# A mixture-of-experts encoder on one core: the last item's rows stay on chip, a zeroed row table, and ones-products ahead of the first transposes

## What is computed

```python
for i in range(DEPTH):                       # DEPTH = 2
    h = rmsnorm(x, norm_mix_g[i])
    x = x + (sgu_mixer(...) if i % 2 == 0 else pool_mixer(...))
    h = rmsnorm(x, norm_ffn_g[i])
    x = x + hierarchical_moe(h, ...)         # hid = silu(xb @ w_gate[e]) * (xb @ w_up[e]); hid @ w_down[e]
return rmsnorm(x, final_norm_g)
# end of hierarchical_moe: every token sums its two experts' rows, each times its gate weight
out = jax.ops.segment_sum(y_sorted * w_sorted[:, None], tok, num_segments=n_tok)
```

## Time and profile before

| | |
|---|---|
| time, median of 3 runs | 2081.47 us (2078.33 to 2082.1) |
| profiled execution: its time, its span | 2081.68 us, 2080.0 us |
| PE busy | 2022.5 us, 97% |
| DVE, ACT, POOL busy | 1576.7, 1363.6, 301.8 us |
| DMA | 559.38 MB, mean 269 GB/s |
| mean granted clock of TensorE | 0.984 |

### The profile page before, as it was taken

The page is one execution under the profiler, slowest core; times in us unless marked ns, Lnnn a source line. Parts: engine busy times, 40 slices in busy tenths (PEclk is TensorE's granted clock), DMA queues, the critical chain, the costliest instruction groups (busy, mean ns, idle before and its releaser), DMA issues.

```text
span 2080.0 us, 31898 instructions
## 1 busy us (share of the span) xinstructions
PE 2022.5 (97%) x9663; PEld 1680.3 (81%) x9663; DVE 1576.7 (76%) x1933; ACT 1363.6 (66%) x1744; POOL 301.8 (15%) x343
## 2 busy tenths in 40 slices
PE   8999999999999999999999989998899999999996
PEld 6888888888788888888888868887688888888883
DVE  4334553426579999999999986867899999999995
ACT  4442244434438888888888874325688888888884
POOL 1000000000002322222222200000133222222110
PEclk9999999999989999999999989998899999999999
DMA  7322223323449999999999983243799999999996
GB/s 278 100 93 81 82 91 101 94 91 116 148 164 348 385 384 377 387 388 371 379 382 384 393 311 137 90 151 132 287 347 378 380 381 382 375 379 385 397 366 260
DMA packets 163754, 559.38 MB, mean 269 GB/s; under 512 B 28472, under 2 KB 29728, under 8 KB 161648
## 3 DMA queue, kind: packets, MB, share of 16 engines
q1 hardware_dynamic: 138960, 510.72, 64.8%
q0 software_dynamic: 22416, 39.30, 5.3%
q10 hardware_dynamic: 2320, 8.62, 1.1%
HBM read 541.21 MB, written 51.97 MB: 285 GB/s over the span
## 4 chain that ended last, share of the span: by engine, by line
PE 90%; DVE 5%; DMA 2%; ACT 1%; issue 1%; SPq 0%; ACTq 0%; DVEq 0%; POOLq 0%
PE bank L628 28%; PE bank L630 27%; PE bank L629 27%; PE bank L893 3%; PE bank L708 2%; PE bank L931 1%; DMA sbias<-y_rows 1%; PE bank L751 1%; PE bank L642 1%; DVE big L1490 1%; DVE w_lo L1482 1%; ACT w_hi L1069 0%; DMA raw<-in_a_w_out 0%; DVE vbias L1540 0%; PE bank L697 0%
## 5 line engine op out<-in xcount | busy, mean ns | idle before, releaser
L628 PE MATMUL bank<-w_hi,a_hi 128*128 128x512 f32 x2072 | 822.3, 397 | 6.1 <-DVE a_lo L1482 2.5
L630 PE MATMUL bank<-w_hi,a_lo 128*128 128x512 f32 x2072 | 809.8, 391 | 0.0
L629 PE MATMUL bank<-w_lo,a_hi 128*128 128x512 f32 x2072 | 807.2, 390 | 0.0
L1482 DVE TENSOR_TENSOR w_lo<-raw,w_hi 128x1024 fp32r<-128x1024 f32 x372 | 454.4, 1225 | 333.8 <-ACT w_hi L1069 308.8
L1069 ACT ACTIVATE w_hi<-raw 128x1024 fp32r<-128x1024 f32 x372 | 392.9, 1060 | 436.7 <-PE bank L630 421.9
L1482 DVE TENSOR_TENSOR w_lo<-big,w_hi 128x1024 fp32r<-128x1024 f32 x530 | 620.0, 1219 | 26.3 <-ACT w_hi L1069 20.8
L1069 ACT ACTIVATE w_hi<-big 128x1024 fp32r<-128x1024 f32 x530 | 549.4, 1063 | 107.6 <-PE bank L630 91.7
L628 PEld LDWEIGHTS bank<-w_hi,a_hi 128*128 128x128 f32 x2072 | 390.4, 188 | 85.2 <-issue 3.3
L630 PEld LDWEIGHTS bank<-w_hi,a_lo 128*128 128x128 f32 x2072 | 389.3, 188 | 83.8
L629 PEld LDWEIGHTS bank<-w_lo,a_hi 128*128 128x128 f32 x2072 | 390.2, 188 | 77.4
L1482 DVE TENSOR_TENSOR a_lo<-bank,a_hi 128x512 fp32r<-128x512 f32 x211 | 137.7, 683 | 32.5 <-ACT a_hi L1069 32.5
(11 more groups left out here) (222 smaller groups left out, 1589.1 us busy)
## 6 DMA issues: line engine op xcount, KB each, us to landing
big<-in_w_gate SPq DMA_DIRECT2D x260, 512.0 KB, 5.7
big<-in_w_up SPq DMA_DIRECT2D x254, 512.0 KB, 5.6
raw<-in_w_down SPq DMA_DIRECT2D x244, 512.0 KB
raw<-in_a_w_in SPq DMA_DIRECT2D x64, 512.0 KB, 3.9
raw<-in_a_w_out SPq DMA_DIRECT2D x32, 512.0 KB, 3.3
big<-y_rows SPq DMA_DIRECT2D x12, 1024.0 KB, 7.3
big<-in_w_down SPq DMA_DIRECT2D x16, 512.0 KB
raw<-in_b_w_in SPq DMA_DIRECT2D x16, 512.0 KB, 4.4
```

What stands on the lines that cost most here:

```text
L628: pe.matmul(dst, left_hi, right_hi, start=first, stop=False)
L629: pe.matmul(dst, left_hi, right_lo, start=False, stop=False)
L630: return pe.matmul(dst, left_lo, right_hi, start=False, stop=last)
L1482: return nc.vector.tensor_tensor(dst, src, f32(hi), ALU.subtract)
```

## The change

1. Layer 1's last item is no longer scattered. Its rows stay in SBUF as `last_hi` (ACT) and `last_lo` (DVE). DVE compares an index row, which PE makes as ones times `tri` in bank 7, with each row's token number and writes eight 0/1 matrices of 128x128, `last_oh`. PE multiplies them with the rows for each of the eight tiles (`add_last`).
2. In layer 1 SP's pair loads wait for the last but one item's scatter. As the last item's rows are then missing from `y_rows`, ACT fills the whole of `y_rows[1]` with zeros early in the kernel.
3. `PE_TILES` are now 1, 3, 4, 6, 7 and `DVE_TILES` 0, 2, 5. Tiles 6 and 7 reuse banks of tiles 1 and 3.
4. PE makes 60 products of ones at the start. For that `tri` holds ones at first; its true values are cast later, ahead of the second round's evictions. The identity is loaded alone, and the rest of `cf` goes on SP's queue behind x.
5. The pooling mixer uses the semaphores of the SGU's ring.

```diff
-PE_TILES, PE_PAIR = (1, 3, 5, 6), (0, 6, 2, 4)
-DVE_TILES = (0, 2, 4, 7)
+PE_TILES, PE_PAIR = (1, 3, 4, 6, 7), (0, 6, 2, 0, 6)
+DVE_TILES, DVE_PAIR = (0, 2, 5), 4
+WARM = 60
...
+            sp.dma_start(cf[:, P:C_ALL], A["c_float"][:, P:C_ALL]).then_inc(g.consts, 16)
...
-                sp.wait_ge(M.scattered, 16 * n)
+                sp.wait_ge(M.scattered, 16 * n if L == 0 else 16 * (n - 1))
+                if L == 1:
+                    sp.wait_ge(M.lo, ROUND * n)
...
+            pool.memset(zeros, 0.0).then_inc(g.init, 1)
...
-                scatter_rows(n - 1, meta_g, end_y)
+                if L == 0:
+                    scatter_rows(n - 1, meta_g, end_y)
...
-            pe.wait_ge(g.consts, 16)
-            pe.wait_ge(g.gain_first, 16)
+            pe.wait_ge(g.eps, 2)
+            for _ in range(WARM):
+                pe.matmul(bank[6][:, 0:P], tri[:, :], tri[:, :], start=True, stop=True)
+            pe.wait_ge(g.gain_first, 32)
...
+                if L == 1:
+                    pe.matmul(bank[7][:, 0:P], ones[:, :], tri[:, :], start=True, stop=True).then_inc(g.iota, 1)
                 down(n - 1, lambda j: pe.wait_ge(M.lo, ROUND * n + j + 1), end_h_hi, end_h_lo, 4)
...
+            def add_last(b, t, first):
+                for c in range(2):
+                    for part in (last_hi, last_lo):
+                        done = pe.matmul(bank[b + c][:, :], last_oh[:, t * P:(t + 1) * P], part[:, c, :],
+                                         start=first and part is last_hi, stop=part is last_lo)
+                return done
...
+            for i in range(3):
+                begin_sum(i)
+            pe.wait_ge(g.moved, TT + 2)
+            for t in range(TT):
+                if t in DVE_TILES:
+                    d = DVE_TILES.index(t)
+                    if d:
+                        pe.wait_ge(g.d_added, 2 * d)
+                    add_last(DVE_PAIR, t, True).then_inc(g.pe_summed, 1)
+                else:
+                    i = PE_TILES.index(t)
+                    if i > 2:
+                        begin_sum(i)
+                    landed, count = pair_landed(1, t)
+                    upper, lower = pair_rows(1, t)
+                    pe.wait_ge(landed, count)
+                    add_rows(PE_PAIR[i], False, False, upper)
+                    add_rows(PE_PAIR[i], False, False, lower)
+                    add_last(PE_PAIR[i], t, False).then_inc(g.pe_summed, 1)
...
-            act.dma_start(cf[:, :], A["c_float"]).then_inc(g.consts, 16)
+            act.dma_start(ident, A["c_float"][:, C_ID:C_ID + P]).then_inc(g.gain_first, 16)
...
+                if hf == 0:
+                    act.wait_ge(g.init, 3)
+                    act.dma_start(y_rows[1].rearrange("(a p) d -> p a d", p=P),
+                                  zeros.rearrange("p (o d) -> p o d", o=1).to_broadcast([P, 2 * TT, D])).then_inc(g.zeroed, 16)
...
-                weighted_rows(end_y, 4, meta_g)
+                weighted_rows(end_y if L == 0 else last_hi, 4, meta_g)
...
+                        if hf == 0:
+                            dve.wait_ge(g.consts, 16)
+                            nc.vector.tensor_copy(tri[:, :], cf[:, C_TRI:C_TRI + P]).then_inc(g.cast, 1)
+                            dve.wait_ge(g.cast, 1)
...
+                    for t in range(TT):
+                        nc.vector.tensor_scalar(last_oh[:, t * P:(t + 1) * P], bank[7][:, 0:P], tile_token[:, t:t + 1], None, ALU.is_equal) \
+                            .then_inc(g.moved, 1)
+                    for c in range(2):
+                        dve.wait_ge(M.y_out, 2 * (n - 1) + c + 1)
+                        nc.vector.scalar_tensor_tensor(last_lo[:, c, :], bank[4 + c][:, :], meta_g[:, 2:3].bitcast(F32), f32(last_hi[:, c, :]),
+                                                       ALU.mult, ALU.subtract).then_inc(g.moved, 1)
```

More of the change, by code:

```diff
@@ L157, in encoder_trunk @@
         end_y = xg.rearrange("p (n f) -> p n f", n=2)
+        last_hi, last_lo = a_hi[:, 3:5, :], a_lo[:, 3:5, :]
+        last_oh = a_hi[:, 5:7, :].rearrange("p a t -> p (a t)")
+        last_token, tile_token = cols[:, 16:17], cols[:, 24:24 + TT]
+        zeros = bu[:, 1024:2048]
         moe_raw = [bu[:, n * UNIT:(n + 1) * UNIT] for n in range(GU)] + [raw[:, n, :] for n in range(DN)]
@@ L243, in encoder_trunk @@
                        "eps", "sq", "std", "rstd", "waited", "hn", "t_full", "t_hi", "t_lo", "out_stored", "last_dn",
-                       "pe_summed", "pe_added",
+                       "pe_summed", "pe_added", "zeroed", "iota", "moved", "d_added",
                        "fold_raw", "fold_left", "fold_hi", "fold_lo", "fold_full", "fold_out", "fold_stored"],
@@ L250, in encoder_trunk @@
                  {"raw": RING})
-        q = sems("pool", RINGS + ["full", "ev_act", "ev_dve", "chain", "d_ready", "d_hi", "d_lo"],
-                 {"raw": RING})
+        q = sems("pool", RINGS + ["full", "ev_act", "ev_dve", "chain", "d_ready", "d_hi", "d_lo"], {})
         ROUTE = ["rw_ready", "x_t", "lg_full", "lg_read", "slots", "slot_oh", "ids_full", "first", "w_full", "tab", "weighted",
@@ L1045, in add_rows, with begin_sum @@
                 return done
-            for b, t in zip(PE_PAIR, PE_TILES):
-                if b == 2:
-                    pe.wait_ge(m[1].y_out, 2 * (n - 1))
[L1050 to L1058, removed]
+            def add_last(b, t, first):
[4 more added lines that the diff above has]
+                return done
+            def begin_sum(i):
+                if i == 1:
+                    pe.wait_ge(g.moved, TT)
+                if i == 2:
+                    pe.wait_ge(m[1].y_out, 2 * (n - 1))
+                if i > 2:
+                    pe.wait_ge(g.pe_added, 2 * (i - 2))
+                add_rows(PE_PAIR[i], True, False, x_res[:, PE_TILES[i], :])
+            for i in range(3):
[9 more added lines that the diff above has]
+                    i = PE_TILES.index(t)
+                    if i > 2:
+                        begin_sum(i)
[5 more added lines that the diff above has]
+                    add_last(PE_PAIR[i], t, False).then_inc(g.pe_summed, 1)
         Q_V = HALVES * BF
@@ L1071, in split @@
             def split(M, slot_raw, slot, src, loads, used):
-                act.wait_ge(M.raw[slot_raw], 16 * loads)
+                act.wait_ge(s.raw[slot_raw], 16 * loads)
                 act.wait_ge(M.used, used)
@@ L1174, in _ @@
                 root(0, t)
-            act.wait_ge(g.gain_first, 18)
+            act.wait_ge(g.gain_first, 34)
             for hf in range(HALVES):
@@ L1714, in _ @@
             nc.vector.memset(eps, EPS).then_inc(g.eps, 1)
[L1715 to L1718, removed]
+            nc.vector.memset(tri[:, :], 1.0).then_inc(g.eps, 1)
+            dve.wait_ge(g.gain_first, 33)
             nc.vector.tensor_copy(mix_gain, bank[7][:, 0:KC]).then_inc(g.gain_first, 1)
-            dve.wait_ge(g.gain_first, 18)
+            dve.wait_ge(g.gain_first, 34)
             dve.sem_inc(s.ev_dve, BANKS)
@@ L2101, in _, with add_last, norm_last @@
             dve.wait_ge(g.gain_ready, 16 * 4)
[L2102 to L2107, removed]
+            def add_last(t):
+                d = DVE_TILES.index(t)
+                dve.wait_ge(g.pe_summed, t + 1)
+                for c in range(2):
+                    x = x_res[:, t, c * 512:(c + 1) * 512]
+                    nc.vector.tensor_tensor(x, bank[DVE_PAIR + c][:, :], x, ALU.add).then_inc(g.d_added, 1)
+                dve.wait_ge(g.d_added, 2 * d + 2)
+            def norm_last(t):
+                normed_tile(8 + t // HT, t // HT, t // HT * HT, t % HT, t // HT)
+            add_last(0)
+            add(1, 0)
+            add_last(2)
+            norm_last(0)
+            add(1, 2)
+            norm_last(1)
+            norm_last(2)
+            add_last(5)
+            norm_last(3)
+            norm_last(4)
+            add(1, 5)
+            for t in (5, 6, 7):
+                norm_last(t)
 _SHAPES = ((1, SEQ, D), "float32")
```

17 lines of the change are left out of this document (12 added, 5 removed).

## The result

The changed kernel takes 2083.22 us (median of 22 runs, 2078.64 to 2085.76), the kernel before 2080.55 us (22 runs on the same chips, 2078.33 to 2082.51). The ratio is 1.0012 with a 95% interval of 1.0006 to 1.0017: 2.7 us slower, under the 0.2% that the forecast called no change. The forecast was 2091 us. The profiled execution has a span of 2081.9 us, 2080.0 before. TensorE (PE) was busy for 98% of it.

What follows compares the result with a forecast made beforehand. PE, busy for 97% of the span, was taken as the bound. 2080.0 - 1.8 (start) + 6.9 (stall) + 1.5 (half clock) + 3.0 (end) = 2089.6 of span, so 2091 us; the range takes in 2081.5 and 2095.

Steps and rivals of the forecast that it cites:

- So I let it go first: Near 20 us: the 8.39 MB zeros store takes all DMA engines for 20.5 us ahead of SP's loads; unit 10 lands at 61.
- +6.9 us of stall: Second round of the main loop: PE wants the bank at 58.3, free only at 65.2; range 6.6 to 9.2.
- +1.5 of half clock: Behind PE's stall: half the clock for 3.0 us, as after the old end's 5.8 us of idling, loses 1.5 us.
- The row that I trusted: Old profile, 547 to 550.5 us: all 290 data packets were a 2 MB store's; a 512 KB load came after it.
- The row at 630.5 to 633.5: Old profile, equal 512 KB pieces: the queues shared, ACT's having 44.0% of the engines' time; cited for even sharing.
- Start, -1.8: Kernel start: ones-products quicken the transposes, moving PE's first main-loop product from 16.56 to about 14.8; 0 to -2.3 us.
- End, +3.0: Last item: loads start 5.4 us sooner, but PE's 27.5 us of sums make scaling end at 2079.3; range 2 to 4.5.
- the queues share evenly: Rival, near 20 us: SP's loads are through by 54, just in time for 58.3, no stall; 2082.9 us, chance 0.30.
- the forecast's main path: Near 20 to 65 us: zeros first, with the PE stall, giving a slower kernel at 2091 us; chance 0.64.
- Decides at an identity sum under 0.64: Faster rival, kernel end: PE's chain under 22 us keeps the tail's 5.4 us; 2074.5 us, chance 0.06 with others under 2077.

Runs made afterwards that it cites:

- e7: The changed kernel itself, profiled once more without an edit: 2081.42 us, one run.
- e1: The kernel before with only the start part of the change, no zeros store and the old end: 2078.48 us, ratio 0.9989.
- e4: The changed kernel with the last sums split 4 and 4 tiles between PE and DVE: 2084.31 us, ratio 1.0021.
- e2: The changed kernel with the zeros store issued behind the first v tiles (about 66 us), not behind the third unit: 2081.32 us, ratio 1.0007.
- e9: The kernel before with only the memset, the zeros store behind ACT's third unit and its wait: 2082.27 us, ratio 1.0004.
- e8: The changed kernel with late zeros, last sums split 4 and 4, and DVE's steps reordered; no GpSimd additions: 2078.61 us, ratio 0.9983.
- e5: The changed kernel with late zeros, 4 and 4 split, DVE's steps reordered, and GpSimd doing DVE's first addition per tile: 2076.43 us, ratio 0.998.
- e6: The changed kernel with the zeros stored by four 2 MB stores, not one of 8 MB, same place: 2088.82 us, one run.

## Why the prediction was wrong

The step that failed is "So I let it go first". It priced the store of zeros at +6.9 us of stall and +1.5 of half clock. The traces show no precedence: the store shares from its first packets on (88 to 68 in the 4 us in which it begins, then 145 to 145, later 210 to 214), unit 10 at 55.6 to 56.2 and not at 61, and a stall of 2.1 to 2.4 us (0.2 where PE was late for another reason). The half clock behind it cost 1.6 us in one execution and nothing in another. At (b) the store costs 2.4 (e7 against e1) to 4.0 us (e4 against e1), not 8.4. The rule of the Trainium skill that the prediction set aside ("DMA: Bandwidth & Descriptors", Queues, rings and completion order: the engines go round robin between queues) is the one that the packets follow.

The row that I trusted was read too far. It was a stretch of 3.5 us right behind the issue of a single load, at 546.23, whose first packets came behind 550.5; it showed a start that was over 4 us late, and the forecast made it 20 us. e2 tells the two apart: its load began over 4 us behind its issue too, but with over 20 us of the store to come. The row at 630.5 to 633.5, with work in both queues, had the answer, 44.0%. Why a transfer starts so late beside a busy queue no run here shows.

The other steps:

- *Start, -1.8:* 2.1 us at (b), inside its range. That the pace of the products brings it is wrong for the most part: without them the loss is 0.3 us. The products were over at 6.4 us and not 8.1. And the start was priced as independent of the zeros. It isn't: e9 and e7 show that the same store costs 0.5 us behind the old start and 2.4 behind the new one.
- *End, +3.0:* (d)-(c) is 42.2 for 39.2, +3.0 (2.1 to 3.1 with the spread of the old end), from a chain of 27.3 us (27.5 forecast) that has no gap from tile 1 on. The way from the last scaling to the end of the span was 3.0 us, not the 3.7 as before, so the span has +2.4 of it. The medians of e2 and e1 differ by 2.8.
- *The rival "the queues share evenly"* gave 2082.9, and its mechanism is the measured one. It put unit 10 "just in time"; it was some 2 us late, as the store began at 23.1 us and not at about 20. That 2082.9 lies so near 2083.22 is in part luck: it is a change of +1.2 us on an execution of 2081.68, and the measured one is +2.7 on a median of 2080.55. The median lies inside the stated range because its low end was drawn for this rival, not because the forecast's main path held.
- *"Decides at an identity sum under 0.64":* the other way out of the chain, fewer sums on PE, was not among the rivals. e8 and e5 take it.

By the differences of the medians: start -2.1 (e1), zeros +1.9 (changed less e2), end +2.8 (e2 less e1). That they add up to the measured change is no test, as each starts where the one before ends. Each is good to about 2 us by the intervals; the positions in the traces are the better evidence.

## What to carry to other kernels

A transfer that nobody waits for still takes its turn at every DMA engine; put it where the engines have time to spare (here 48 us later in the program), not where a free source first allows it. When two edits meet at one landing, don't add their prices: work out when each side arrives, and take the later. And when a wait for data is taken away at the end of a kernel, count every engine's remaining work first: here the loads came over 5 us earlier, and even the best end (e5) took 38.2 us where the old one took 39.1 to 40.1, and only with the sums spread over PE and DVE and an order that let DVE work during ACT's roots.

## What was unexpected of the hardware

- A transfer issued beside a busy queue had its first packets over 4 us later (546.23 before, 18.86 in the changed kernel, 69.74 in e2), where the engines were idle about 1 us later (66.79 in e2). Then the queues shared evenly.
- Four stores of 2 MB, issued one behind the other, held ACT for 13.70 us; one of 8 MB, the same rows in all, held it 0.39 us (e6 and the changed kernel).
- The clock was low from 14.9 to 18.2 us in one of eight executions that had the products at the start, and after an idle of 2.1 to 2.4 us at 60 us in one of two (e4, not e7). Here a stall's half clock was a chance, not a term with a fixed price.
- Three DVE instructions of 1.2 to 1.3 us took 2.1 to 3.2 us while GpSimd added two SBUF operands in e5; those that read a PSUM bank did not slow down.
